# A long layer kernel with a rebuilt beginning, a re-cut attention inner product, column-packed modulation products and later column sums

## The reference, cut to what matters

```python
def stick_breaking_attention(xn, w_qkv, w_o):
...
        z = jnp.einsum('bthd,bshd->bhts', qb, kb)
...
        log_1m = jnp.where(mask, jax.nn.log_sigmoid(-z), 0.0)
        log_w = jax.nn.log_sigmoid(z) + lax.cumsum(log_1m, axis=3, reverse=True) - log_1m
        w = jnp.where(mask, jnp.exp(log_w), 0.0)
...
        mod = jax.nn.silu(c) @ w_mod[layer] + b_mod[layer]
...
        mod_c = jax.nn.silu(c_ctx) @ w_mod[layer] + b_mod[layer]
```

## Time and profile before

| | us |
|---|---|
| three runs | 1733.19, 1733.65, 1732.93 (median 1733.19) |
| the profiled execution | 1732.6, its span 1730.8 |
| PE busy | 1671.6 (97%) |
| DVE busy | 1230.7 (71%) |
| ACT busy | 850.8 (49%) |
| POOL busy | 104.3 (6%) |

### The profile page before, as it was taken

How to read it: one execution, slowest core, us unless ns; L and a number is a source line. 1 busy time by engine, 2 the same in 40 slices (tenths; PEclk the granted TensorE clock), 3 DMA queues, 4 the chain that set the end, 5 groups by cost and what they waited for, 6 DMA issues and landing times.

```text
span 1730.8 us, 34493 instructions
## 1 busy us (share of the span) xinstructions
PE 1671.6 (97%) x14503; PEld 1592.4 (92%) x14503; DVE 1230.7 (71%) x1583; ACT 850.8 (49%) x977; POOL 104.3 (6%) x103
## 2 busy tenths in 40 slices
PE   7999999999999998899999999999999999899998
PEld 7989999999999995699999998999998769889998
DVE  6846777887887877857777785778776676654445
ACT  5455545646445541354555545555554643353333
POOL 1002000004500012100000000200000000000000
PEclk9999999999999999999999999999999999999999
DMA  8804555544445533454555690545543132045552
GB/s 328 327 34 151 189 177 189 201 169 171 171 170 180 185 123 120 151 171 159 182 185 179 252 348 33 188 170 179 184 170 104 41 123 98 30 167 175 189 177 91
DMA packets 40499, 286.77 MB, mean 166 GB/s; under 512 B 4624, under 2 KB 4624, under 8 KB 6224
## 3 DMA queue, kind: packets, MB, share of 16 engines
q1 hardware_dynamic: 39456, 280.99, 45.1%
q10 hardware_dynamic: 944, 4.33, 0.7%
HBM read 284.25 MB, written 1.05 MB: 165 GB/s over the span
## 4 chain that ended last, share of the span: by engine, by line
PE 68%; DVE 14%; ACT 9%; issue 7%; POOL 1%; DVEq 0%; ACTq 0%; DMA 0%; POOLq 0%; SPq 0%
PE PS L1922 19%; PE PS L1923 19%; PE PS L1924 19%; ACT whi L407 5%; DVE AR L1233 4%; DVE wlo L1003 4%; ACT AR L524 2%; PE PS L2244 1%; PE PS L1936 1%; PE PS L2222 1%; PE PS L2258 1%; PE PS L2611 1%; PE PS L2048 1%; POOL AR L2754 1%; PE PS L2388 0%
## 5 line engine op out<-in xcount | busy, mean ns | idle before, releaser
L1922 PE MATMUL PS<-XH,whi 128*128 128x256 f32 (+1 forms) x2824 | 817.7, 290 | 16.8 <-DVE wlo L1003 8.4
L1923 PE MATMUL PS<-XL,whi 128*128 128x256 f32 (+1 forms) x2824 | 809.7, 287 | 0.0
L1924 PE MATMUL PS<-XH,wlo 128*128 128x256 f32 (+1 forms) x2824 | 809.5, 287 | 0.0
L1003 DVE TENSOR_TENSOR wlo<-raw,whi 128x2048 fp32r<-128x2048 f32 x240 | 551.6, 2300 | 167.4 <-ACT whi L407 167.2
L1922 PEld LDWEIGHTS PS<-XH,whi 128*128 128x128 f32 x2824 | 543.9, 193 | 28.4 <-issue 12.7
L1923 PEld LDWEIGHTS PS<-XL,whi 128*128 128x128 f32 x2824 | 544.2, 193 | 3.7 <-issue 0.5
L1924 PEld LDWEIGHTS PS<-XH,wlo 128*128 128x128 f32 x2824 | 544.1, 193 | 3.3
L407 ACT ACTIVATE whi<-raw 128x2048 fp32r<-128x2048 f32 x240 | 456.3, 1902 | 59.1 <-PE PS L1924 48.7
L1922 PE MATMUL PS<-HH,whi 128*128 128x256 f32 x756 | 215.2, 285 | 4.5 <-DVE wlo L1003 2.7
L1923 PE MATMUL PS<-HL,whi 128*128 128x256 f32 x756 | 214.4, 284 | 0.0
L1924 PE MATMUL PS<-HH,wlo 128*128 128x256 f32 x756 | 214.3, 283 | 0.0
(11 more groups left out here) (386 smaller groups left out, 1498.4 us busy)
## 6 DMA issues: line engine op xcount, KB each, us to landing
raw<-wst SPq DMA_DIRECT2D x248, 1024.0 KB, 4.8
AR<-mst SPq DMA_DIRECT2D x17, 1024.0 KB, 6.6
XT<-x_in SPq DMA_DIRECT2D x2, 512.0 KB, 5.8
AR<-crow ACTq DMA_DIRECT2D x2, 512.0 KB, 5.5
AR<-sbc ACTq DMA_DIRECT2D x1, 1024.0 KB, 6.4
AR<-ctxin ACTq DMA_DIRECT2D x1, 1024.0 KB, 6.7
y_out<-XT SPq DMA_DIRECT2D x4, 256.0 KB, 2.4
AR<-sgw ACTq DMA_DIRECT2D x1, 512.0 KB, 3.5
```

The lines of the kernel that those rows point to most:

```text
L1003: dve.tensor_tensor(wlo[:, r, :], raw[:, u % RING, :], whi[:, r, :].bitcast(F32), ALU.subtract)\
L1922: pe.matmul(dst, sh, mh, start=first, stop=False, **kw)
L1923: pe.matmul(dst, sh, ml, start=False, stop=False, **kw)
L1924: return pe.matmul(dst, sl, mh, start=False, stop=last, **kw)
```

## The change

Five edits at once.

1. **Beginning.** Unit 0 is loaded and split in halves; ACT loads a function table before it waits for x; the squares of the last four tiles come behind the split of unit 1; PE multiplies 18 times a tile of zeros (512 columns, bf16) before the first real product; units 0, 1 and 2 are multiplied part by part, first all of `whi` with `XH`, then `whi` with `XL`, then `wlo` with `XH`; unit 0 gets bank 0, so that PE waits for a taken bank from the fourth unit on and no longer from the third.
2. **Places of the sums.** For parts 1, 3, 5 and 7 both products of `scale_sums` come four k-steps (12 matmuls) later; for part 0 the first comes behind unit 1, the second inside unit 2.
3. **Attention.** `bounded` and its buffer go. ACT takes exp straight from PSUM, DVE does min and max in one instruction, then writes the result as a rounded part and a rest into halves of a free slot of `whi` and `wlo`. PE multiplies both parts with `NUR`, a rounded copy of `negU`, in one pass each and 384 columns; only `negones` stays plain f32. The slot is that of the unit after next, so the split of the second output unit moves: on ACT to the end of step 8, on DVE behind the loop.
4. **Modulation.** Each product of 256 columns becomes four of 64 columns that go to four different groups of 32 PSUM partitions; DVE adds the bias in four instructions instead of one.
5. **Semaphores.** Several load semaphores are merged; the same transfers are waited for.

```diff
@@ scale_sums and its table
+SUMS_AT = {0: (1, 1, 7), 2: (0, 1, 3), 4: (0, 1, 3), 6: (0, 1, 3)}
...
-                if (unit, m, k) == ((0, 1, 3) if t.free else (1, 0, KT - 1)):
-                    tiles, t.rows = ((0, 1, 6, 7), (1, 3)) if t.free in BEHIND_FFN else ((0, 1), (0, 3) if t.free else (1, 5))
+                if (unit, m, k) == SUMS_AT.get(t.free, (0, 1, 7)):
+                    tiles, t.rows = ((0, 1, 6, 7), (1, 3)) if t.free in BEHIND_FFN else ((0, 1), (0, 7))
@@ first units, PE
+                for half, hi, lo in ((0, "first_hi", "first_lo"), (1, "w_hi", "w_lo")):
+                    ks = range(4 * half, 4 * half + 4)
+                    pe.wait_ge(S["op_hi"], 4 * half + 4)
+                    pe.wait_ge(S[hi], 1)
+                    unit_part(b, whi[:, 0], XH, ks, first=half == 0)
+                    pe.wait_ge(S["op_lo"], 4 * half + 4)
+                    unit_part(b, whi[:, 0], XL, ks)
+                    pe.wait_ge(S[lo], 1)
+                    mm = unit_part(b, wlo[:, 0], XH, ks, last=half == 1)
...
+            pe.wait_ge(S["setup"], 1)
+            for _ in range(18):
+                pe.matmul(PS[:, 7, :], IDB[:, :], IDB[:, :].unsqueeze(1).broadcast_to([P, 4, P]), start=True, stop=True)
@@ fresh_bank
-                if t.pp >= 2:
+                if t.pp >= 3:
                     pe.wait_ge(S["pp_taken"], t.pp - 1)
                 t.pp += 1
-                return 4 + (t.pp - 1) % 2
+                return 4 + (t.pp - 1) % 2 if t.pp > 1 else 0
@@ attention, DVE
+                    dve.scalar_tensor_tensor(SP[:, p % 2, :].rearrange("p (a b) -> p a b", a=2),
+                                             LN[:, p % 2, :].rearrange("p (a b) -> p a b", a=2), 40.0,
+                                             PS[:, 2 * r:2 * r + 2, 0:384], ALU.min, ALU.max).then_inc(S["sp_ready"], 1)
...
+                    dve.tensor_copy(whi[:, slot, c], SP[:, p % 2, :]).then_inc(S["sp_high"], 1)
+                    dve.wait_ge(S["sp_high"], n0 + p + 1)
+                    dve.tensor_tensor(wlo[:, slot, c], SP[:, p % 2, :], whi[:, slot, c].bitcast(F32), ALU.subtract)\
+                        .then_inc(S["sp_low"], 1)
@@ attention, PE
-                        pe.wait_ge(S["sp_ready"], n0 + p)
-                        for i in range(2):
-                            b = PS[:, 2 * r + i, :]
-                            s = SP[:, (p - 1) % 2, 384 * i:384 * i + 384]
-                            pe.matmul(b[:, 0:T], negU, s[:, 0:T], start=False, stop=True, **kw)
-                            pe.matmul(b[:, P:T], negones, s[:, T:T + P], start=False, stop=True, **kw)
-                            mm = pe.matmul(b[:, T:T + P], negU, s[:, T:T + P], start=False, stop=True, **kw)
+                        for part, ready in ((whi, "sp_high"), (wlo, "sp_low")):
+                            pe.wait_ge(S[ready], n0 + p)
+                            for i in range(2):
+                                o = 768 * ((p - 1) % 2) + 384 * i
+                                mm = pe.matmul(PS[:, 2 * r + i, 0:384], NUR[:, :], part[:, slot, o:o + 384],
+                                               start=False, stop=True, **kw)
@@ modulation, PE
-                    mm = pe.matmul(PS[32 * (g // 2):32 * (g // 2) + 32, bank, (g % 2) * 256:(g % 2) * 256 + 256],
-                                   SCP[:, k, :], raw[:, t.u % RING, k * 256:(k + 1) * 256],
-                                   start=(k == 0), stop=(k == KT - 1))
+                    for c in range(4):
+                        r, o = 32 * (c ^ (g % 2)), P * (g // 2) + 64 * (c % 2)
+                        mm = pe.matmul(PS[r:r + 32, bank, o:o + 64], SCP[:, k, :],
+                                       raw[:, t.u % RING, k * 256 + 64 * c:k * 256 + 64 * c + 64],
+                                       start=(k == 0), stop=(k == KT - 1))
```

More of the change, by code:

```diff
@@ L407, in split_hi, with ahead @@
                 act.activation(whi[:, r, :], raw[:, u % RING, :], ACT.Copy).then_inc(S["w_hi"], 1)
-            def ahead(u):
-                while t.s < limit(u) and t.s <= split_index(u) + 2:
+            def ahead(u, most=2):
+                while t.s < limit(u) and t.s <= split_index(u) + most:
                     split_hi(t.s)
@@ L627, in attention @@
                 for n in range(4):
-                    ahead(t.u)
+                    ahead(t.u, 2 if n < 3 else 1)
                     if n == 3:
@@ L1987, in features, with early_unit @@
+            def early_unit(b, u):
+                pe.wait_ge(S["w_hi"], u + 1)
+                unit_part(b, whi[:, u], XH, range(KT), first=True)
+                unit_part(b, whi[:, u], XL, range(KT))
+                if u == 2:
+                    scale_sums(2, 0, 0)
+                pe.wait_ge(S["w_lo"], u + 1)
+                unit_part(b, wlo[:, u], XH, range(KT), last=True).then_inc(S["w_used"], 1)
+                if u == 1:
+                    scale_sums(1, 1, KT - 1)
             def features(first=False, per=1, at=0, scales=None):
@@ L2050, in scale_sums @@
                     mm.then_inc(S["col_sum"], 1)
-                if (unit, m, k) == (1, *t.rows):
+                if (unit, m, k) == ((1, *t.rows) if t.free else (2, 0, 0)):
                     pe.wait_ge(S["diag_ready"], t.free + 1)
```

161 lines of the change are left out of this document (88 added, 73 removed).

## The result

| | before | changed |
|---|---|---|
| median of the runs | 1733.06 us (4 runs, 1732.46 to 1733.65) | 1716.74 us (4 runs, 1715.28 to 1717.57) |
| profiled execution, its span | 1732.6, 1730.8 | 1715.28, 1713.4 |
| ratio of changed to before | | 0.9903, 95% interval 0.9887 to 0.9919 |

The change gains 16.3 us by the medians and 17.4 us by the two spans. The forecast was 1710.7 with a range of 1700 to 1720: the sign and the range hold, the size was 6 us too hopeful.

The account below looks back on a forecast made before the run. PE, busy 97% of the span, was taken as the bound, with other limits where edits apply. Gains 2.6 + 9.0 + 3.4 + 7.5 = 22.5 us off 1732.6 gave 1710.1, as a median 1710.7; range 1700 to 1720.

Parts of the forecast that it names:

- What bounds the kernel: Whole kernel: PE, busy 97% of the span; a change pays where it shortens PE-bound stretches or PE's waits.
- Beginning: Start to unit 3: earlier first product and full clock, limited by DVE's second take; 2.6 us gained, bounds 0.9 to 4.7.
- if those 2 us drop it again: Beginning's low bound: PE's idling of some 2 us ahead of unit 3 lowers the clock, leaving 0.9 us gained.
- Attention: Both attentions: a loop step falls from 4.0 to 3.45 us; 4.5 us gained in each, 9.0 together.
- the latency of two steps: Attention loop: the chain through scores and sums takes 6.9 us for two steps, 3.45 each, against PE's own 3.26.
- Places of the sums: Parts 1, 3 and 7 gain 1.6 us each, part 5 loses 1.4; sum 3.4, bounds 1.0 to 6.0.
- Modulation and state space: State-space layer: units of 1.0 us instead of 3.62, DVE the next limit; 7.5 us gained, bounds 4.0 to 10.4.
- ahead of step 2: State-space layer: PE done at 662.1, DVE going on around 663; 4.5 us gained of DVE's 7.59 wait.
- the waits ahead of steps 4 and 6: State-space layer: DVE's waits of 1.37 and 1.55 us, from gaps in `outputs`, become hidden; 2.9 us gained.
- Idle PE turns slow: Rival, chance 0.17: idling of 1 to 5 us brings slow stretches in four places; gain 15 us, 1718.
- The four column groups take turns: Rival, chance 0.03, modulation: groups share one stationary tile, each record loads its own; at 0.17 us a record 1763.
- More comes through: Rival, chance 0.14: attentions reach PE's own bound (12.0), ffn entries 5, modulation 9, beginning 4; gain 30 us, 1703.

Follow-up runs that it names:

- e1_attention: The kernel before with the attention edit alone: median 1726.25 us, ratio to before 0.9972.
- e4_beginning: The kernel before with only the new beginning, part 0's sums and the merged load semaphores: median 1731.85 us, ratio to before 0.9998.
- e10_one_group: The changed kernel with each modulation unit's 64 records in one column group and DVE's bias as one addition: 1724.28 us, ratio to before 0.9948.

## Why the prediction was right in sign and 6 us off

- **What bounds the kernel.** Right: PE's work pays where PE bounds a stretch. PE still has 68% of the chain.
- **Beginning, forecast 2.6, measured 0.5.** The mechanism was right up to unit 3: first product 8.54 (8.3 forecast), a wait of 2.13 for DVE's second take, unit 3 at 29.71 (29.1), so 2.0 to 2.4 us. The step that failed is the choice between the bounds: the prediction named "if those 2 us drop it again", priced it at 1.7, and left it out of the sum. It came in 3 of 6 traces with that wait, so half of its price belonged in the sum, and filling the wait took it away.
- **Attention, forecast 9.0, measured 7.3.** The limit named, the latency of two steps, was right, and the double CAST confirmed it (0.22 of 0.28). The size was off in each term by a little. First attention: first sums 0.59 (0.74 forecast), six steps 3.1 (3.4; before's first two steps were 3.94 and 3.98, not 4.05), last sums 0.60 (0.7), waiting behind the loop 0.45 (0.3). In the second attention the second sums come 2.71 after the first ones instead of 2.33, and it gives 3.5.
- **Places of the sums, forecast 3.4, measured about 4 against this profile of before.** 1.6 in part 1, 1.5 in part 3 and 0.84 behind it (not taken apart), 1.5 in part 7, and -1.4 in part 5. The numbers agree, and so does the reading that DVE's chain keeps its 16.2 us and the rest becomes a wait of 1.4 at the first down product. What failed is the premise that a slow stretch follows the wait each time. All of the 1.5 is that stretch, which comes in 8 of 12 cases, so the three parts are worth some 3.1 in the mean and not 4.6 (`e1_attention`, `e4_beginning`).
- **Modulation and state space, forecast 7.5, measured 7.6 against this profile of before.** 4.5 was forecast ahead of step 2, and 5.2 came; the other two waits nearly went, as forecast. That the total agrees is luck: the profile of before was 2.6 to 3.8 us slower here than three other kernels with the same modulation, a second execution of the changed kernel gains 5.0, and the average against the average is 4.1. So this term was mis-sized too, 7.5 for 4.1, though the ledger hid it. Where the prediction takes the waits ahead of steps 4 and 6 (1.37 and 1.55) as a cost that before always has, the three other kernels show 0.9 and 0.7, none and 1.2, and none at all. The prediction also lets the slow clock work on the first units from 652.0, but they start at 652.77, which makes 4.1 of its 4.5. Behind the last `outputs` another 0.7 went: the slow stretch from 702.88 reaches 1.5 us past them into the next products.
- **The end, forecast nothing, measured -1.2.** Left out altogether: where nothing is changed, two traces still differ. Before's profile had two slow stretches in the second network, the changed one three. The waits near 1485 and 1511 that precede two of them were in the trace of before too, and all but one of the 24 such unfilled waits were followed by a stretch: it was before that was lucky.
- **Rivals.** "Idle PE turns slow" (0.17) was right for the beginning. In the modulation the idle times did bring half clock, 23.9 us of it instead of 13.7, but in a stage that DVE bounds. At the new waits of 1.41 ahead of the down products no stretch followed. "The four column groups take turns" is refuted by `e10_one_group`: turns are what it shows, at 57 ns. "More comes through" fails on the chains of DVE and ACT.
- **The whole.** The single edits add up to 9 us by their ratios and all together give 16.8, which the theory of independent parts doesn't explain.
- **What is open.** Why the edits are worth more together than alone. Why the clock falls behind an idle time in one execution and not in the next wasn't found, nor was what PE waits for in the gaps of 1 to 4 us inside `outputs`, modulation and `own_pair` that the profile puts down to nothing; they come at other places in every execution, and those of over 0.9 us in this stage add up to 7.5 to 15.3 us with four column groups and to 0 to 5.9 with the old modulation.

## What to carry to other kernels

Give a slow stretch behind an idle time a rate, not a yes or no, and look at several traces before you count it as cost or as gain: a removed wait may be worth only the stretch that it brings. One profile of the kernel before can be slow at the very place that you change; the profiles of kernels that leave that place alone are the better measure. When work is taken off an engine, work out the latency of the loop around it over as many steps as are in flight, since that, and not the engine's remaining work, may set the new step. A known idle time of PE outside a latency-bound stage can be filled with products that nobody reads, if they surely end before the wait does.

## What the runs showed of the hardware that was not expected

- The same kernel on the same chip, 31 times, took 1726.5 to 1735.6 us, with a mean granted clock of 0.993 in the fastest and 0.988 in the slowest. 0.005 of 1730 us is 8.7 us, near the spread of 9.1. It isn't all: the nine runs at 0.990 range over 4.5 us.
- Small products on four column groups start 16 ns apart on average, on one group 57 ns, with the same operands.
- Eight one-column products and a wait of 1.26 us ahead of them were followed by a slow stretch in 8 of 12 cases, a wait of 2.13 in 3 of 6, one of 3.55 in 11 of 12 and one of 2.69 in 12 of 12. The places of the last three waits, filled with unused products, had none in 7 cases.
- At the start the products of zeros and the first real products of before run at half the later pace, while the profile's granted clock stands at 1.00 over these windows (0.00:8.50 of the changed kernel, 10.00:13.70 of before). There only the pace shows it.
- The CAST of 768 numbers from f32 to the rounded type takes 0.56, the subtraction of as many 0.96. ACT's exp straight from PSUM takes 0.81, from SBUF it took 0.84.
